# A three-product fp32 split in a transformer trunk: high weights against high and low activations in one product

## The chip, the cores and the metric

One core of one Trainium2 chip. The metric is the device time of one execution in microseconds; the lower the better.

## The reference

A trunk of two layers on one sequence of 256 tokens, width 1024, in float32. Each layer has a mixer with three branches, merged by gates, and then a SwiGLU: dense in layer 0, top 2 of 8 experts in layer 1.

```python
for l in range(DEPTH):
    h = rmsnorm(x, g_mix[l])
    p = h @ w_in[l]
    c_q, c_kv, k_r, z_sg, q_x, gate_logits = jnp.split(p, SPLITS, axis=-1)
    y_a = mla_branch(c_q, c_kv, k_r, ...)          # latent self-attention, 8 heads
    y_b = spatial_gating_branch(z_sg, ...)         # u * (w_s @ rmsnorm(v) + b_s), u, v = split(gelu(z_sg))
    y_c = memory_branch(q_x, mem_n, w_mkv[l])      # 4 heads over 256 memory rows
    yd = jnp.einsum('bsnw,nwd->bsnd', jnp.stack([y_a, y_b, y_c], axis=2), w_br[l])
    gates = jax.nn.sigmoid(gate_logits.reshape(b, s, N_BRANCH, d) + b_gate[l])
    x = x + jnp.sum(gates * yd, axis=2) @ w_out[l]
    h = rmsnorm(x, g_ffn[l])
    x = x + (swiglu(h, ...) if l % 2 == 0 else moe_swiglu(h, ...))
return rmsnorm(x, g_final)
```

## The kernel before, in words

**Precision.** Large weights and their activations are split: the high part is a copy to float32r (ScalarE, L1219), the low part is the value less its high part (VectorE, L1567). A product is the sum of three: high x high, weights high x activations low, weights low x activations high (`acc3`, L594). Activations stand transposed in `hT`, two tiles `hT_hi` and `hT_lo` of 128 x 8 x 256; `mT` and `yT` are alike. In the transposed products (gates, su, qx, dense up) a block of 128 x 128 weights is stationary and 256 tokens move through, three times for each of 8 blocks of rows.

**Weights.** They come in pieces of 1 MB into slots of `raw` (3 slots in the mixer, 7 else), one piece behind the other in the order of `pieces` (L424 on; there `su` is the first half u of the spatial branch's input, `sv` its half v, `qx` the memory branch's query, `gate` and `br` the gates and projections of a branch n, w1, w3, w2 the dense weights). A slot is loaded again when the low part of its old piece is made. `whi` and `wlo` have 3 slots (SPLIT): piece m needs the products of piece m - 3 done. `room(name)` (L534) counts the pieces whose slots come free by marks before the mark of `name`; ScalarE and VectorE call `hi_parts(room(...))` and `lo_parts(room(...))` at fixed places of their in-order programs, and wait there for the release.

**PSUM.** `plan_psum` (L61) hands out the banks at build time: in the mixer six in rotation (0 to 3, 6, 7), in the dense stage four for the up projections. `claim` waits on TensorE until the last group in that bank has been read, `full` waits for a product, `read` for the reader of a bank.

**Order of a layer's mixer on TensorE.** cq, ckv, sv (tokens as rows), then su and qx (`transposed`, L675), spatial matrices, latent transposes, latent products q (L730). Then `mixer_steps` (L156), an order written by hand. Memory attention, i = 0 to 5: scores ms(i), at i = 0 also k and v; transposed probabilities mpT(i - 1), values mo(i - 2), and one unit (1, i). Then transposes qT and kT. Self-attention, i = 0 to 9: scores as(i), apT(i - 1), O(i - 2), and a unit: (1, 6), (1, 7), (2, 0) to (2, 7). Last oT and the units of branch 0, (0, 0) to (0, 7), and the output product.

**A unit** (n, d) (L732) is channel block d of branch n: a gate product of 24 matmuls and a projection of 12, side by side in one bank; gate first, but for d = 3 and 7, where the projection is first. ScalarE takes the tanh of the gate from PSUM (L1326), VectorE merges in the same step: (tanh + 1) x projection (L1733), and for n != 1 adds it to the sum (L1737); for n = 0 it also splits the sum (L1739, L1740). `sig` and the temporary have two buffers. In the memory steps VectorE also makes the row maximum of the scores (L1752), scales the probabilities (L1760), makes the low half of a value (L1771) and rotates the queries and keys (L1716 to L1721).

**Dense stage** (L864): for each b two chunks of 128 hidden channels; a chunk is a w1 and a w3 product in the halves of one bank; silu on ScalarE (L1399), product and split on VectorE (L1842 to L1844); then the down product of block b - 1. Behind it comes the expert stage (L975 to L1007), which takes over half of the time.

## Time and profile before

| what | value |
|---|---|
| median of 3 runs (lowest to highest) | 1710.83 us (1710.59 to 1711.66) |
| profiled execution, own time | 1712.28 us |
| its span, first to last instruction | 1710.5 us |
| mean granted TensorE clock | 0.995 |
| share of the chain that ended last on TensorE | 95% |

The sum of a prediction is made against the profiled execution, 1712.28 us, which is 1.45 us over the median; 1.8 us of it lie around the span. Durations of matmuls in a profile overlap, so the distance between two starts is what one costs in a row.

### The profile page before, as it was taken

What the parts mean: (1) busy time and instruction counts of PE and PEld (TensorE: products, weight loads), DVE (VectorE), ACT (ScalarE), POOL (GpSimd) and SP (SyncE); (2) the same over time, 40 slices, a digit from 0 to 9 for tenths busy, and PEclk for the clock granted to TensorE, in tenths of its full rate; (3) what the DMA queues carried; (4) which work ended last, traced back from release to release, by engine and by line L of the source; (5) the groups of instructions that cost most, each with busy time, mean ns of one, the idle gap of its engine ahead of it and who ended that gap; (6) DMA issues with size and microseconds to landing.
All of it is one profiled execution on the core that took longest, in us unless ns stands there. A gap on an engine that the chain in (4) does not pass through costs nothing.

```text
span 1710.5 us, 24615 instructions
## 1 busy us (share of the span) xinstructions
PE 1668.2 (98%) x9340; PEld 1449.8 (85%) x9340; DVE 1283.9 (75%) x1221; ACT 1051.2 (61%) x965; POOL 18.3 (1%) x44
## 2 busy tenths in 40 slices
PE   7999999999999999999999999999999999999996
PEld 6989998999988999888888888888888888888885
DVE  6655575655565556678888888888888888888996
ACT  5534544433453454457777777777777777777774
POOL 1000000000000000000000000000000000000100
PEclk9999999999999999999999999999999999999998
DMA  8633449885473335769999999999999999999992
GB/s 277 199 123 100 123 148 354 302 262 177 157 219 125 123 115 170 260 244 385 354 388 390 357 387 390 355 397 385 364 393 377 364 392 362 386 391 358 393 394 110
DMA packets 252569, 493.96 MB, mean 289 GB/s; under 512 B 8310, under 2 KB 86720, under 8 KB 252496
## 3 DMA queue, kind: packets, MB, share of 16 engines
q1 hardware_dynamic: 247424, 479.23, 78.3%
q10 hardware_dynamic: 3664, 9.44, 1.4%
q0 software_dynamic: 1408, 4.28, 0.7%
q8 instruction: 50, 0.82, 0.2%
q14 instruction: 23, 0.19, 0.0%
HBM read 473.52 MB, written 19.40 MB: 288 GB/s over the span
## 4 chain that ended last, share of the span: by engine, by line
PE 95%; DVE 2%; issue 1%; ACT 1%; DMA 0%; DVEq 0%; ACTq 0%; SPq 0%
PE bank L601 34%; PE bank L975 24%; PE bank L1007 18%; PE bank L979 12%; PE bank L591 3%; PE bank L992 1%; PE bank L825 1%; PE bank L796 1%; PE bank L639 1%; DVE wlo L1567 0%; PE bank L778 0%; PE bank L1019 0%; PE bank L651 0%; DMA hn<-in_mem 0%; ACT pbuf L1232 0%
## 5 line engine op out<-in xcount | busy, mean ns | idle before, releaser
L1924 DVE TENSOR_TENSOR wlo<-raw,whi 128x2048 fp32r<-128x2048 f32 x328 | 748.1, 2288 | 108.9 <-ACT whi L1432 108.7
L1432 ACT ACTIVATE whi<-raw 128x2048 fp32r<-128x2048 f32 x328 | 627.8, 1919 | 179.5 <-PE bank L979 94.2
L1567 DVE TENSOR_TENSOR wlo<-raw,whi 128x2048 fp32r<-128x2048 f32 (+3 forms) x113 | 249.3, 2210 | 196.7 <-ACT whi L1219 196.5
L975 PE MATMUL bank<-whi,yT_hi 128*128 128x512 f32 x896 | 354.3, 395 | 0.8 <-issue 0.8
L975 PE MATMUL bank<-whi,yT_lo 128*128 128x512 f32 x896 | 349.3, 390 | 0.0
L1219 ACT ACTIVATE whi<-raw 128x2048 fp32r<-128x2048 f32 (+3 forms) x113 | 209.0, 1851 | 131.9 <-PE bank L601 114.1
L601 PE MATMUL bank<-hT_hi,whi 128*128 128x256 f32 x848 | 243.7, 287 | 3.1 <-DVE hT_lo L1589 1.8
L979 PE MATMUL bank<-wlo,yT_hi 128*128 128x512 f32 x896 | 240.0, 390 | 0.0
L601 PE MATMUL bank<-hT_hi,wlo 128*128 128x256 f32 x848 | 239.9, 283 | 0.0
L601 PE MATMUL bank<-hT_lo,whi 128*128 128x256 f32 x848 | 239.8, 283 | 0.0
L979 PEld LDWEIGHTS bank<-wlo,yT_hi 128*128 128x128 f32 x896 | 168.2, 188 | 35.6
L975 PEld LDWEIGHTS bank<-whi,yT_hi 128*128 128x128 f32 x896 | 168.3, 188 | 34.5 <-issue 0.9
L975 PEld LDWEIGHTS bank<-whi,yT_lo 128*128 128x128 f32 x896 | 168.4, 188 | 33.5
L1007 PE MATMUL bank<-whi,yT_hi 128*128 128x512 f32 x448 | 176.4, 394 | 3.4 <-DVE yT_lo L1939 2.4
L1007 PE MATMUL bank<-wlo,yT_hi 128*128 128x512 f32 x448 | 175.2, 391 | 0.0
L1007 PE MATMUL bank<-whi,yT_lo 128*128 128x512 f32 x448 | 175.1, 391 | 0.0
L601 PEld LDWEIGHTS bank<-hT_hi,whi 128*128 128x128 f32 x848 | 162.5, 192 | 4.6 <-issue 2.0
L601 PEld LDWEIGHTS bank<-hT_lo,whi 128*128 128x128 f32 x848 | 162.5, 192 | 1.1 <-issue 0.5
L601 PEld LDWEIGHTS bank<-hT_hi,wlo 128*128 128x128 f32 x848 | 162.4, 192 | 0.0
L1007 PEld LDWEIGHTS bank<-whi,yT_hi 128*128 128x128 f32 x448 | 84.4, 188 | 28.3 <-issue 8.6
L1007 PEld LDWEIGHTS bank<-wlo,yT_hi 128*128 128x128 f32 x448 | 84.5, 189 | 18.0
L1007 PEld LDWEIGHTS bank<-whi,yT_lo 128*128 128x128 f32 x448 | 84.6, 189 | 16.3
(263 smaller groups left out, 1788.7 us busy)
## 6 DMA issues: line engine op xcount, KB each, us to landing
raw<-in_moe_w SPq DMA_DIRECT2D x336, 1024.0 KB, 7.5
raw<-in_w_in SPq DMA_DIRECT2D x36, 1024.0 KB, 5.3
raw<-in_dense_w SPq DMA_DIRECT2D x30, 1024.0 KB, 8.0
raw<-in_w_br SPq DMA_DIRECT2D x12, 1024.0 KB, 5.1
raw<-in_w_mkv SPq DMA_DIRECT2D x8, 1024.0 KB, 6.4
raw<-in_w_out SPq DMA_DIRECT2D x8, 1024.0 KB, 5.0
rows_by_slot<-qxT SPq DMA_DIRECT2D x15, 512.0 KB, 8.8
y_by_slot<-qxT SPq DMA_DIRECT2D x9, 512.0 KB, 8.4
```

The lines of the kernel that those rows point to most:

```text
L591: ins = nc.tensor.matmul(bank, lhs(k), rhs(k), start=(k == 0), stop=(k == n - 1))
L601: ins = nc.tensor.matmul(bank, lhs(a, k), rhs(b, k), start=(start and k == chunks[0] and a + b == 0), stop=(stop and k == chunks[-1] and a ...
L639: nc.tensor.matmul(b[:, 0:P], ident[:, :], ident[:, :], start=True, stop=True)
L796: ins = nc.tensor.transpose(b[:, a:a + P], prob[:, nth % 2, t, tok(kt)], ident[:, :])
L825: ins = nc.tensor.matmul(b[:, t * SEQ:(t + 1) * SEQ], qT[0:QK, h, tok(t)], kT[0:QK, h, :], start=True, stop=True)
L975: nc.tensor.matmul(b[:, :], hselT[a][:, half, tok(k)], w[:, k, :], start=(half + k + a == 0), stop=False)
L979: ins = nc.tensor.matmul(b[:, :], hselT[0][:, half, tok(k)], w[:, k, :], start=False, stop=(half == 1 and k == 3))
L1007: ins = nc.tensor.matmul(banks[4 + n][:, :], gated_m[a][:, tok(2 * half + c)], w[p][:, c, n * HALF:(n + 1) * HALF], start=(b_ + half + c + ...
L1219: nc.scalar.activation(whi[:, m % SPLIT, 0:floats(n)], raw[:, pieces[n][1], 0:floats(n)], ACT.Copy).then_inc(hi_ready, 1)
L1432: nc.scalar.activation(whi[:, (E0 + n) % SPLIT, :], raw[:, n % RAW, :], ACT.Copy).then_inc(hi_ready, 1)
L1567: V.tensor_tensor(wlo[:, m % SPLIT, 0:size], raw[:, pieces[n][1], 0:size], whi[:, m % SPLIT, 0:size].bitcast(F32), ALU.subtract).then_inc( ...
L1924: V.tensor_tensor(wlo[:, s, :], raw[:, n % RAW, :], whi[:, s, :].bitcast(F32), ALU.subtract).then_inc(lo_ready, 1)
```

## The change

The high weights of a block are multiplied with high and low activations at once: the two halves stand side by side in one tile `hT`, and move as 512 columns; the low weights' 256-column product is added to the first half of the bank. A product so fills a whole bank, and VectorE adds the bank's halves into SBUF. This is done for su, qx, the gates and dense w1 and w3. gelu, tanh and silu then read the sum from SBUF. A unit takes two banks, and its merge on VectorE is put behind the work of the next step (`waiting`), in branch 0 behind the next unit's add. `down` waits for the new semaphore `gated_ready`. The views of `hT` for the expert stage are laid out anew. Diff, cut:

```diff
+    def take_unit(l, n, d):
+        for name in ("unit", "gate") if d % 4 == 3 else ("gate", "unit"):
+            take((name, l, n, d))
...
-            for t in range(2):
+            for t in range(4 if name in ("su", "qx") else 2):
                 take((name, l, t))
...
+                take(("up1", l, c), among=(0, 1, 2, 3))
                 take(("up", l, c), among=(0, 1, 2, 3))
...
-        hT = [sb(f"hT_{i}", [P, KD, SEQ], F32R) for i in ("hi", "lo")]
+        hT_both = sb("hT", [P, KD, 2, SEQ], F32R)
+        hT = [hT_both[:, :, i, :] for i in range(2)]
...
+        gate_sum = cT[:, 3:5, :]
...
+            def acc_pair(bank, w, cc, norm=None):
+                for k in range(KD):
+                    if norm is not None and k % 2 == 0:
+                        read(pe, ("nT", norm, k // 2))
+                    nc.tensor.matmul(bank[:, :], w[0][:, k, tok(cc)], hT_both[:, k, :, :].rearrange("p a s -> p (a s)"),
+                                     start=(k == 0), stop=False)
+                    ins = nc.tensor.matmul(bank[:, 0:SEQ], w[1][:, k, tok(cc)], hT[0][:, k, :],
+                                           start=False, stop=(k == KD - 1))
+                return ins
...
-                transposed("su", hT)
-                transposed("qx", hT)
+                for name in ("su", "qx"):
+                    for i in range(4):
+                        if i % 2 == 0:
+                            w = weight((name, l, i // 2), KD)
+                        ins = acc_pair(claim((name, l, i)), w, i % 2)
+                        mark(ins, (name, l, i), *([("piece", name, l, i // 2)] if i % 2 else []))
...
                     def gate():
                         w = weight(("gate", l, n, d // 2), KD)
-                        return acc3(b[:, 0:SEQ], lambda a, k: w[a][:, k, tok(d % 2)], lambda a, k: hT[a][:, k, :],
-                                    range(KD), True, True)
+                        ins = acc_pair(claim(("gate", l, n, d)), w, d % 2)
+                        mark(ins, ("gate", l, n, d), *([("piece", "gate", l, n, d // 2)] if d % 2 else []))
...
@@ ScalarE
-                for n in range(2):
-                    hi_parts(room(("su", l, n)))
-                    b = full(act, ("su", l, n))
...
+                for i in range(4):
+                    hi_parts(room(("su", l, i)))
+                    read(act, ("su", l, i))
+                    nc.scalar.activation(uT[:, i, :], uT[:, i, :], ACT.Gelu_apprx_tanh).then_inc(u_ready, 1)
+                for i in range(4):
+                    hi_parts(room(("qx", l, i)))
...
-                    b = full(act, ("unit", l, n, d))
+                    read(act, ("gate", l, n, d))
...
-                        hi_parts(room(name))
+                        hi_parts(room(("gate",) + name[1:] if kind == "unit" else name))
...
+                        hi_parts(room(("up1", l, c)))
+                        read(act, ("up1", l, c))
+                        nc.scalar.activation(silu_d[:, c % 4, :], silu_d[:, c % 4, :], ACT.Silu).then_inc(silu_ready, 1)
                         hi_parts(room(("up", l, c)))
...
@@ VectorE
+            def add_halves(dst, name):
+                b = full(dve, name)
+                free(V.tensor_reduce(dst, b[:, :].rearrange("p (a s) -> p s a", a=2), AX_X, ALU.add), name)
...
+                for i in range(4):
+                    lo_parts(room(("su", l, i)))
+                    add_halves(uT[:, i, :], ("su", l, i))
+                for i in range(4):
+                    lo_parts(room(("qx", l, i)))
                     if l:
                         dve.wait_ge(zeroed, 16 * N_ZEROED)
-                    free(V.tensor_copy(qxT[:, 2 * n:2 * n + 2, :].rearrange("p h s -> p (h s)"), b[:, :]), ("qx", l, n))
+                    add_halves(qxT[:, i, :], ("qx", l, i))
...
+                def unit_gate(n, d):
+                    lo_parts(room(("gate", l, n, d)))
+                    add_halves(gate_sum[:, (units + len(waiting)) % 2, :], ("gate", l, n, d))
+                    waiting.append((n, d))
+                def merge_waiting():
+                    while waiting:
+                        lo_parts(room(("unit", l) + waiting[0]))
+                        unit_merge(*waiting.pop(0))
...
-                    if kind not in ("O", "ms", "as", "k"):
+                    if kind not in ("O", "ms", "as", "k", "unit"):
                         lo_parts(room(name))
...
-                        unit_merge(*step[1:])
+                        unit_gate(*step[1:])
+                        continue
...
+                    merge_waiting()
+                merge_waiting()
...
                 for d in range(KD):
-                    lo_parts(room(("unit", l, 0, d)))
-                    unit_merge(0, d)
+                    unit_gate(0, d)
+                    if d:
+                        lo_parts(room(("unit", l) + waiting[0]))
+                        unit_merge(*waiting.pop(0))
+                merge_waiting()
...
+                        lo_parts(room(("up1", l, c)))
+                        add_halves(silu_d[:, c % 4, :], ("up1", l, c))
                         lo_parts(room(("up", l, c)))
...
-                        link(V.tensor_tensor(g, silu_d[:, c % 4, :], b[:, SEQ:2 * SEQ], ALU.mult))
+                        add_halves(g, ("up", l, c))
+                        read(dve, ("up", l, c))
+                        dve.wait_ge(silu_ready, c + 1)
+                        link(V.tensor_tensor(g, g, silu_d[:, c % 4, :], ALU.mult))
```

## Rows read from the trace of the kernel before

**Rows 1.** The page, part 1 (busy time) and part 6 (loads, last number us to landing).
```profile
PE 1668.2 (98%) x9340; PEld 1449.8 (85%) x9340; DVE 1283.9 (75%) x1221; ACT 1051.2 (61%) x965; POOL 18.3 (1%) x44
...
raw<-in_w_br SPq DMA_DIRECT2D x12, 1024.0 KB, 5.1
```

**Rows 2.** The chain that ended last, first 760 us (start, length, what; x counts instructions).
```profile
151.68 4.32 PE bank L601 x36
...
156.00 0.87 PE bank L825 x4
...
212.39 56.50 PE bank L601 x384
...
326.25 155.46 PE bank L601 x1068
...
484.82 48.91 PE bank L601 x336
...
537.04 7.84 PE bank L591 x24
```

**Rows 3.** Groups by line and form, the 256-column product of high and high.
```profile
L601 PE MATMUL bank<-hT_hi,whi 128*128 128x256 f32 x848 | 243.7, 287 | 3.1 <-DVE hT_lo L1589 1.8 <-DVE mT_lo L1589 1.3
```

**Rows 4.** TensorE's timeline (start, length, what), 24 products of 512 columns between the two.
```profile
337.84 0.40 PE L601 MATMUL bank<-whi,yT_hi 128*128 128x512 f32 x1
...
343.30 0.28 PE L601 MATMUL bank<-hT_hi,whi 128*128 128x256 f32 x1
```

**Rows 5.** VectorE's timeline, layer 1, around the qx projection.
```profile
519.90 2.28 DVE L1567 TENSOR_TENSOR wlo<-raw,whi 128x2048 fp32r<-128x2048 f32 x1
...
534.64 2.05 DVE L1686 TENSOR_SCALAR cT<-bank,cols 128x256 f32<-128x256 f32 x5 [0.18 <-PE bank L632]
```

**Rows 6.** VectorE's timeline, layer 0, first mixer steps.
```profile
123.98 0.68 DVE L1752 TENSOR_REDUCE rmax<-bank 128x2 f32<-128x512 f32 x1
...
126.79 0.42 DVE L1771 TENSOR_TENSOR yT_lo<-bank,yT_hi 128x256 fp32r<-128x256 f32 x1
...
128.46 0.41 DVE L1733 SCALAR_TENSOR_TENSOR hn<-cT,bank 128x256 f32<-128x256 f32 x1
...
145.18 2.29 DVE L1567 TENSOR_TENSOR wlo<-raw,whi 128x2048 fp32r<-128x2048 f32 x1 [3.78 <-ACT whi L1219]
...
147.39 0.41 DVE L1733 SCALAR_TENSOR_TENSOR hn<-cT,bank 128x256 f32<-128x256 f32 x1
...
147.72 2.47 DVE L1790 COPY raw<-bank 96x512 f32<-96x512 f32 x4
```

**Rows 7.** ScalarE's timeline, the same steps.
```profile
125.82 0.59 ACT L1350 ACTIVATE pbuf<-bank 128x512 f32<-128x512 f32 x1
...
143.24 1.92 ACT L1219 ACTIVATE whi<-raw 128x2048 fp32r<-128x2048 f32 x1 [2.55 <-PE bank L601]
...
145.06 0.46 ACT L1326 ACTIVATE cT<-bank,half_gate 128x256 f32<-128x256 f32 x1
```

**Rows 8.** TensorE's timeline, from the last of these steps to the first attention scores.
```profile
144.42 2.34 PE L815 MATMUL bank<-ident,raw 128*96 128x128 f32 x20
...
147.86 1.84 PE L815 MATMUL bank<-ident,raw 128*96 128x128 f32 x12 [1.10 <-DVE hn L1733]
...
150.58 1.10 PE L825 MATMUL bank<-raw 96*128 96x256 f32 x4 [0.88 <-ACT raw L1363]
```

**Rows 9.** VectorE's timeline, a merge of branch 0 and the operation behind it.
```profile
231.18 0.41 DVE L1733 SCALAR_TENSOR_TENSOR sgv<-cT,bank 128x256 f32<-128x256 f32 x1
...
232.75 2.28 DVE L1567 TENSOR_TENSOR wlo<-raw,whi 128x2048 fp32r<-128x2048 f32 x1
```

**Rows 10.** Waits, first 760 us (us in all, times, longest).
```profile
PE bank L639 <- DVE hT_lo L1589: 3.5, 1, 3.5
```

**Rows 11.** A stretch around 725 us: busy time of PE, PEld, DVE, ACT, POOL, then granted clock.
```profile
720.00:730.00 10.00, 8.78 (x51) 8.59 (x51) 8.99 (x13) 1.54 (x2) 0.00 (x0) 0.68 0.77 283
```

More of the change, by code:

```diff
@@ L95, in plan_psum @@
         for step in mixer_steps(heads, x_heads):
-            if step[0] != "O":
+            if step[0] == "unit":
+                take_unit(l, *step[1:])
+            elif step[0] != "O":
                 take((step[0], l) + step[1:])
@@ L102, in plan_psum @@
         for d in range(8):
-            take(("unit", l, 0, d))
+            take_unit(l, 0, d)
         for n in range(2):
@@ L1299, in _ @@
                 own_squares()
-                for n in range(2):
-                    hi_parts(room(("su", l, n)))
-                    b = full(act, ("su", l, n))
-                    free(nc.scalar.activation(uT[:, 2 * n:2 * n + 2, :].rearrange("p h s -> p (h s)"), b[:, :],
-                                              ACT.Gelu_apprx_tanh), ("su", l, n))
-                for n in range(2):
-                    hi_parts(room(("qx", l, n)))
+                for i in range(4):
[4 more added lines that the diff above has]
+                    hi_parts(room(("qx", l, i)))
                 hi_parts(room(("wsT", l)))
@@ L1371, in _ @@
                 for d in range(KD):
-                    hi_parts(room(("unit", l, 0, d)))
+                    hi_parts(room(("gate", l, 0, d)))
                     unit_tanh(0, d)
@@ L1689, in _ @@
                 dve.wait_ge(row_in, 16 * (l + 1))
-                for n in range(2):
-                    read(dve, ("su", l, n))
+                dve.wait_ge(u_ready, 4 * (l + 1))
                 for t in range(T):
@@ L1727, in unit_merge @@
                     units += 1
+                    b = full(dve, name)
                     dve.wait_ge(tanh_ready, units)
-                    b = banks[groups[name].bank]
                     s_ = sig[:, (units - 1) % 2, :]
@@ L1732, in unit_merge @@
                     dst = mixT[:, d, :] if first else gated_tmp[:, units % 2, :]
-                    free(V.scalar_tensor_tensor(out=dst, in0=s_, scalar=1.0, in1=b[:, SEQ:2 * SEQ], op0=ALU.add,
+                    free(V.scalar_tensor_tensor(out=dst, in0=s_, scalar=1.0, in1=b[:, 0:SEQ], op0=ALU.add,
                                                 op1=ALU.mult), name)
@@ L1836, in _ @@
                             norm_lo(3 * l + 3, mT, c_of["mem"])
+                        lo_parts(room(("up1", l, c)))
+                        add_halves(silu_d[:, c % 4, :], ("up1", l, c))
                         lo_parts(room(("up", l, c)))
-                        dve.wait_ge(silu_ready, c + 1)
-                        b = banks[groups["up", l, c].bank]
                         g = g32_d[:, c % 2, :]
                         part = [v[:, c // BD % 2, c % BD, :] for v in gated_d]
-                        link(V.tensor_tensor(g, silu_d[:, c % 4, :], b[:, SEQ:2 * SEQ], ALU.mult))
+                        add_halves(g, ("up", l, c))
+                        read(dve, ("up", l, c))
+                        dve.wait_ge(silu_ready, c + 1)
+                        link(V.tensor_tensor(g, g, silu_d[:, c % 4, :], ALU.mult))
                         link(V.tensor_copy(part[0], g))
-                        free(V.tensor_tensor(part[1], g, part[0].bitcast(F32), ALU.subtract), ("up", l, c))
+                        V.tensor_tensor(part[1], g, part[0].bitcast(F32), ALU.subtract).then_inc(gated_ready, 1)
             for t in range(T):
```

52 lines of the change are left out of this document (22 added, 30 removed).

## The prediction, made before the changed kernel ran

> **What bounds the kernel.** I read the page first: TensorE has work for 98% of the span, VectorE 75%, ScalarE 61% [rows 1]. So time can be won only on TensorE, or lost where another engine makes it wait. Next the chain that ended last, over the first 760 us, since the expert loop behind them (L975, L1007) is not touched: in the stages that the change edits, the chain is TensorE's own matmuls end to end; the output and branch-0 stage is one piece of 56.50 us, the dense stage one of 155.46 us [rows 2]. The reader should see there that a stage without a wait gives back exactly what its matmuls get shorter by.
>
> Then the price of a matmul. The group row says 287 ns for a 256-column product, x848 [rows 3], but matmuls overlap: the mean is a latency. The price is the distance between starts. 36 products of 256 columns take 4.32 us [rows 2], 0.120 us each; 24 of 512 columns take 343.30 - 337.84 = 5.46 us [rows 4], 0.2275 us each. So 256 more columns cost 0.1075 us, and each product has some 0.0125 us on top.
>
> **TensorE's part.** Each weight block of 128 rows had three 256-column products, 0.360 us. It gets one of 512 and one of 256, 0.3475 us: 0.0125 us less. There are 848 of them [rows 3]: 336 in the dense up projections (42 products of 8 blocks), 384 in the gates (48), 128 in su and qx (16). That is 848 x 0.0125 = **-10.6 us**, 0.10 us a product of 8 blocks. No row shows 512 and 256 columns in turn. Bounds: 0.333 us a pair if one of the two fixed parts goes (-22.9 us), 0.360 if nothing is won (0). I take 0.3475, since both sizes carry the same fixed part when they follow their own kind. The Trainium skill, "TensorE: Matmul & The Clock Gate", section "Back-to-back issue gap", puts an isolated gap at columns/2.4 + 2.5 ns; by it this sum would be 848 x 2.5 ns = 2.1 us, but both measured distances lie over 10 ns above that formula.
>
> **VectorE's part.** Every one of the 106 products gets an add of halves, a reduction over 512 PSUM elements. The nearest row is the maximum of attention scores, same operand size: 0.68 us long [rows 6], and four copies of this length come every 0.62 us [rows 6]. I take 0.62. Bounds: 0.33, the distance behind a 256-element operation (147.39 to 147.72) [rows 6], and twice 0.68 if the strided read of pairs is slow. qx loses two copies of 0.62 a layer. What counts is where the add stands: ScalarE's tanh, gelu and silu now wait for it, and behind them in ScalarE's queue stand high parts of weights (1.9 us [rows 7]), then in VectorE's queue their low parts (2.2 us from start to start [rows 6]), for which TensorE waits. No DMA is added or moved by itself, but a load waits for the low part of the piece in its slot.
>
> *Dense up projections.* A block of two chunks is 4 x 2.78 + 5.46 = 16.6 us on TensorE. VectorE has 3 x 2.2 low parts, 4 adds, two chains of 1.1: 11.3 us. The first weights' next piece is freed at 8.3 us; add, silu, high and low part end at 13.7, before it is wanted at 16.6. The second pair's is ready 1.7 us early. Four banks hold two chunks. Added work is hidden; cover left is those 1.7 us. Full gain, -4.2 us.
>
> *su and qx.* VectorE is held by the normalisation of v until 519.90 [rows 5]; su's first two products are long done, so adds run at 519.9 to 521.2, gelu to 521.6, and only then ScalarE makes qx's second high part (to 523.5), VectorE its low part (to 525.7). TensorE wants it at 527.3: no wait. But su's other adds and gelus end at 527.4, the first gate piece's high part at 529.3, low part at 531.5, qx's first two adds at 532.7. The first projection piece loads into the slot whose low part ended at 525.7, so 5.1 us later [rows 1]: high part 531 to 533, low part to 535.2, two adds to 536.5. The five latent copies, 2.05 us [rows 5], end at 538.6, and the latent products, which read them and started at 537.04 [rows 2], start at 538.8: **1.8 us later**, the 0.8 us gained included, so 2.6 us of stall.
>
> *First mixer steps, with memory scores.* Two banks a unit instead of one, of six in rotation, and the merge is put behind the next step's scores. Let 0 be the start of the third scores (ms2). TensorE: scores 0.87 [rows 2], transposes, values, gate to 5.0, projection to 6.4; then ms3 wants the bank of unit (1,1). VectorE: maximum to scaled probabilities is 126.79 - 123.98 = 2.8 us [rows 6]; ScalarE is free 1.84 after the maximum started [rows 7], makes the high part freed by gate (1,1) until 4.6, VectorE the low part until 6.9, the merge until 7.3: **0.9 us wait**. Then VectorE runs solid: yT and rotation 1.67 [rows 6], add, ms3's 2.8, merge, yT and rotation, low part to 16.5, add (1,3) to 17.2, tanh 0.46, high part to 19.5, low part to 21.8, merge (1,3) to 22.2. TensorE is at the last values (mo3) at 19.25 and wants just that bank: **3.0 us wait**. Last, gate (1,5) ends at 25.9; VectorE reaches its add at 27.0; tanh, high part, low part, a copy and the merge end at 32.7. TensorE finished five groups of transposes in 2.34 us [rows 8] at 29.65: a wait of 3.05 where 1.10 stood [rows 8]; the scores then follow 0.5 us sooner after it, since copies overlap (before, 150.58 - 147.86 [rows 8]). Stall added: 0.9 + 3.0 + 1.95 - 0.5 = **5.3 us**.
>
> *Self-attention steps.* A step is 6.4 us on TensorE and about 4.3 on VectorE. The same chain makes VectorE at most 2.5 us late, and every bank comes free before its next claim. Nothing added.
>
> *Branch 0.* A unit is 4.2 us on TensorE; on VectorE the merge is 232.75 - 231.18 = 1.57 us [rows 9], add 0.62, three quarters of a low part 1.65: 3.85 us. Played through, it begins with 0.65 us for oT's low half, which now stands behind add and tanh, and ends with the last merge 0.6 us after TensorE wants it: **1.25 us**.
>
> **Sum.** Stalls 2 x (2.6 + 5.3 + 1.25) = 18.3 us, less 10.6: +7.7 us. The profiled execution took 1712.28 us (span 1710.5), so 1720.0; the median of the runs, 1710.83, gives **1718.5 us**. If adds cost 0.33, some six in su and qx, four in the steps and one in branch 0 leave the path, 11 x 0.29 x 2 = 6.4 us: +1.3. If they cost 1.36, +16 more.
>
> **Rivals.** *A: the stalls don't come* because my order of queues is too strict or adds are short. For it: in the dense stage cover is there; against: VectorE already has no gap from 126.79 to 128.46 and behind. Then 1710.83 - 10.6 = 1700.2 us; with half the stalls 1709. Faster by over 0.2% (3.4 us, what a measurement can tell from no change): 0.20, within it 0.13. *B: the clock falls.* The 3.5 us wait [rows 10] was followed by 10 us at a mean granted clock of 0.68, so 6.4 us of them at 1.2 GHz instead of 2.4 [rows 11]; mo3's wait and kT's, four of some 3 us in all, come near it. At 1.2 GHz 256 columns take twice their 0.107, 0.213 us, so such a fall costs 6.4 x (1 - 0.120/0.213) = 2.8 us; after two of the four: 1718.5 + 5.6 = 1724.1. Chance 0.15. *C: no product saving*, the fixed part following columns when sizes alternate: 1718.5 + 10.6 = 1729.1, chance 0.05. The skill's formula above would give 1718.5 + 8.5 = 1727; it is worth 0.02 more, as the rows contradict it.
>
> **Numbers.** My forecast has 0.45 (its own range 1714.3 to 1723), B, C and the formula 0.22, A's faster side 0.20, no change 0.13: slower 0.67. The range, 1702 to 1726, reaches into A up to nearly all its gain and takes in B; outside it stay C and a full A.
>
> **What would show it.** Right: in su, gates and up the two products start 0.347 us apart in pairs; the dense stage is 4.2 us shorter; TensorE waits for merge L1733 or its successor at ms3, mo3 and kT; the latent products start late behind qx's adds. Wrong: adds of under 0.4 or over 1 us, pairs of other length, dense stage with waits, or no wait of TensorE between 92 and 151 us.

## The result, and the profile after

The changed kernel takes 1733.04 us, the median of 4 runs (1732.85 to 1734.85), beside 1710.71 for the kernel before (1709.48 to 1711.66): ratio 1.0132, 95% interval 1.012 to 1.0145, **22.3 us slower**. The sign was forecast; 1718.5 us and the range up to 1726 were too low. The profiled executions differ alike: a span of 1731.3 us beside 1710.5. Of the version best_fill below, one of eleven executions took 3529.7 us; its median, 1708.35, counts it (1707.8 without), its ratio doesn't.

The page of the kernel after: busy time of each engine, with its share of the span.

```profile
PE 1666.3 (96%) x8492; PEld 1404.7 (81%) x8492; DVE 1347.0 (78%) x1323; ACT 1052.9 (61%) x969; POOL 18.1 (1%) x44
...
PE 87%; DVE 7%; ACT 3%; issue 3%; DMA 0%; DVEq 0%; ACTq 0%; SPq 0%
...
L622 PE MATMUL bank<-hT,whi 128*128 128x512 f32 x848 | 308.2, 405 | 3.2 <-DVE hT L1617 1.8
...
L624 PE MATMUL bank<-hT,wlo 128*128 128x256 f32 x848 | 239.1, 282 | 0.0
...
L1348 ACT ACTIVATE cT<-cT,half_gate 128x256 f32<-128x256 f32 x48 | 24.5, 510 | 131.2 <-DVE cT L1597 131.2
```

TensorE, which had work for 98% of the span [rows 1], now has it for 96%. L622 is the wide product, L624 the narrow one, L1597 the add of halves. VectorE and ScalarE together hold a tenth of the chain that ended last, the chain of work in which each piece released the next. ScalarE's tanh stands idle 131 us for the adds; that costs nothing by itself, but weights' high parts are queued behind it.

TensorE's waits of the kernel after, us in total, times and longest:

```profile
PE bank L938 <- DVE qxT L1907: 6.2, 1, 6.2
PE bank L840 <- DVE hn L1774: 5.7, 2, 2.8
PE bank L603 <- DVE hn L1774: 5.5, 2, 2.7
...
PE bank L613 <- DVE yT_lo L1852: 3.1, 2, 1.5
...
PE bank L803 <- DVE hn L1774: 2.0, 2, 1.0
```

Once a layer, TensorE waits for a merge (L1774) at kT (L840, where 1.1 us stood before [rows 8]), at the last value product mo3 (L603), and at the fourth memory scores (L803): the three places forecast. L613 is branch 0's first projection; L938, at the router, comes up in the section on the router.

Where the time went, from the start of the first product of each stage in both traces (`cq` is the first product of a layer's mixer, q the latent products). Both layers are summed; a forecast is stalls less saved product time:

| stage | change, us | forecast |
|---|---|---|
| up to cq of layer 0 | -1.6 | 0 |
| cq to the start of q, with su and qx | +3.0 | +3.6 |
| memory steps, qT and kT, to the first scores | +14.8 | +9.4 |
| self-attention steps | -0.6 | -2.0 |
| branch 0 and output | +4.8 | +0.9 |
| dense stage | -1.9 | -4.2 |
| end of layer 1's output to the first expert | +1.2 | 0 |
| experts | +1.2 | 0 |
| sum | +20.8 | +7.7 |

The experts stage, which no version touches, took between 956.4 and 959.5 us in the traces of this study; differences of its size are no effect. The same holds for the stretch from the first product with weights (15.1 us) to cq of layer 0, which took 26.4 to 28.2 us in this study: in the kernel before TensorE starts 15 products between 14 and 18 us, in the one after 25, at a granted clock of 1.00 in both. Why isn't settled.

### The profile page after: what moved, and what is told of

The parts are those of the page before. It is cut to its first block, busy times and chain, and to the rows that moved or that the text cites. A ratio compares the mean times of both kernels' runs of the same rounds, so it can differ in the third digit from the quotient of the medians.

```text
span 1731.3 us, 23163 instructions
## 1 busy us (share of the span) xinstructions
PE 1666.3 (96%) x8492; PEld 1404.7 (81%) x8492; DVE 1347.0 (78%) x1323; ACT 1052.9 (61%) x969; POOL 18.1 (1%) x44
## 4 chain that ended last, share of the span: by engine, by line
PE 87%; DVE 7%; ACT 3%; issue 3%; DMA 0%; DVEq 0%; ACTq 0%; SPq 0%
PE bank L998 23%; PE bank L1030 18%; PE bank L613 14%; PE bank L1002 12%; PE bank L622 9%; PE bank L624 4%; PE bank L603 3%; ACT whi L1242 2%; DVE wlo L1590 2%; PE bank L1015 1%; PE bank L850 1%; PE bank L821 1%; DVE cT L1597 0%; PE bank L662 0%; DVE pbuf L1597 0%
## 5 line engine op out<-in xcount | busy, mean ns | idle before, releaser
L622 PE MATMUL bank<-hT,whi 128*128 128x512 f32 x848 | 308.2, 405 | 3.2 <-DVE hT L1617 1.8
L624 PE MATMUL bank<-hT,wlo 128*128 128x256 f32 x848 | 239.1, 282 | 0.0
L622 PEld LDWEIGHTS bank<-hT,whi 128*128 128x128 f32 x848 | 160.8, 190 | 41.9 <-DVE wlo L1590 2.3
L624 PEld LDWEIGHTS bank<-hT,wlo 128*128 128x128 f32 x848 | 161.7, 191 | 1.1 <-issue 0.5
L1348 ACT ACTIVATE cT<-cT,half_gate 128x256 f32<-128x256 f32 x48 | 24.5, 510 | 131.2 <-DVE cT L1597 131.2
L1463 ACT ACTIVATE sgv<-bank 128x512 f32<-128x512 f32 x56 | 33.6, 599 | 44.8 <-PE bank L1002 44.7
```

Of the source, the lines that this page charges most:

```text
L622: nc.tensor.matmul(bank[:, :], w[0][:, k, tok(cc)], hT_both[:, k, :, :].rearrange("p a s -> p (a s)"), start=(k == 0), stop=False)
L624: ins = nc.tensor.matmul(bank[:, 0:SEQ], w[1][:, k, tok(cc)], hT[0][:, k, :], start=False, stop=(k == KD - 1))
L1463: free(nc.scalar.activation(silu_m, b[:, :], ACT.Silu), (phase, "e1", b_))
```

## One part at a time: dense, gates, su and qx

The theory going in: TensorE bounds, the stalls come from VectorE's adds and their place in the queues, and the three parts add up. Its rivals: the saving per pair is off, the clock falls cost what is missing, or the parts disturb one another.

```diff
 # dense_only: only these stay as in the change
+    ins = acc_pair(b, w1, cc, ...)
+    ins = acc_pair(b, w3, cc)
 # dense_grouped: besides, in acc_pair
     for k in range(KD):
         nc.tensor.matmul(bank[:, :], w[0][:, k, tok(cc)], hT_both[:, k, :, :]..., start=(k == 0), stop=False)
+    for k in range(KD):
         ins = nc.tensor.matmul(bank[:, 0:SEQ], w[1][:, k, tok(cc)], hT[0][:, k, :], ...)
```

> The 512 + 256 pair and the add of halves in the dense up projections alone; su, qx and gates as before. Theory 1 (the loss sits in the mixer, where adds, high parts and merges stand in line; a pair is 0.353 us and not 0.3475): the dense stage is 336 x 0.007 = 2.3 us shorter, TensorE waits nowhere new, total -1.9 to -2.4 us, ratio 0.9987. Theory 2 (the adds also cost in the dense stage, and the mixer is only part of the loss): 0 to +5 us. Theory 3 (pairs at 0.3475): -4.2 us, ratio 0.9975.

1707.75 us, ratio 0.9984 (0.9975 to 0.9993): faster by 2.9 us. The interval reaches from 1.2 to 4.3 us, so the total can't tell theory 1 from theory 3; the distances in the trace do. Only the dense stage moved. Its part behind the sixth chunk, 240 pairs, became 1.65 us shorter, 0.0069 us a pair, which is theory 1's price. TensorE's rows of one gate in the kernel after show it, here its last four pairs, in order of time:

```profile
209.78 0.40 PE L622 MATMUL bank<-hT,whi 128*128 128x512 f32 x1
210.01 0.28 PE L624 MATMUL bank<-hT,wlo 128*128 128x256 f32 x1
210.12 0.40 PE L622 MATMUL bank<-hT,whi 128*128 128x512 f32 x1
...
210.84 0.40 PE L622 MATMUL bank<-hT,whi 128*128 128x512 f32 x1
211.07 0.28 PE L624 MATMUL bank<-hT,wlo 128*128 128x256 f32 x1
211.19 0.28 PE L613 MATMUL bank<-yT_hi,whi 128*128 128x256 f32 x1
```

Four pairs take 211.19 - 209.78 = 1.41 us, 0.353 each, where 0.3475 was forecast. Over the whole trace the median distance from a wide product's start to the narrow one's is 236 ns, from narrow to the next wide 117.

> As dense_only, but each product runs its eight 512-column matmuls first and then its eight 256-column ones. If the excess of a pair over 0.3475 us comes from alternating sizes (236 + 117 ns where uniform rows show 227 and 120), distances go back to 227 and 120 inside each run of eight and 336 x 0.0055 = 1.8 us more are won than in dense_only: about -4 us. If the excess belongs to the 512-column matmul on the joined tile itself, distances stay at 236 and 117 and the time is that of dense_only.

1707.23 us, ratio 0.9982 (0.9973 to 0.9991). Two groups of eight in this kernel:

```profile
347.03 2.00 PE L621 MATMUL bank<-hT,whi 128*128 128x512 f32 x8
348.87 1.11 PE L624 MATMUL bank<-hT,wlo 128*128 128x256 f32 x8
349.82 2.00 PE L621 MATMUL bank<-hT,whi 128*128 128x512 f32 x8
```

(349.82 - 347.03) / 8 = 0.349 us a pair; eight wide ones alone 1.84 / 8 = 0.230. The same part of the stage is 2.74 us shorter, 0.0114 a pair. So equal widths in a row keep nearly the price of uniform rows, and the change of width within the pair cost the difference. The two totals can't be told apart; the stage shows it. Both kernels lose 0.8 and 1.5 us in the first six chunks, where the granted clock fell for 3.4 us at 278 us behind the norm's wait, and did not in the kernel before. So the traced executions show less of the gain than the medians; that of dense_only was the longest of eleven, 1710.66 us.

```diff
 # gates_only: the change's gates and their merge order; dense, su, qx as before
+    ins = acc_pair(claim(("gate", l, n, d)), w, d % 2)
```

> Pair, add, two banks a unit and late merge for the gates alone; su, qx and dense as before. Theory 1: the waits at ms3, mo3 and kT, those around branch 0 and the clock falls behind them are all here: 2 x (1.1 + 2.9 + 1.7) + 2 x 2.6 in waits, 3 clock falls of 1.5, less 384 x 0.007 = 2.7: +18 to +20 us of the +22, ratio 1.011. Theory 2: well under half of it, below +11.

1729.92 us, ratio 1.0114 (1.0099 to 1.013), 19.3 us slower than before. Per layer: memory steps +5.4, transposes +1.5, self-attention -0.3, branch 0 +1.2, its last units and the output +1.3. **The gates are nearly the whole loss**, and their waits are those of the full change:

```profile
PE bank L834 <- DVE hn L1771: 5.7, 2, 2.8
PE bank L602 <- DVE hn L1771: 5.6, 2, 2.9
...
PE bank L612 <- DVE yT_lo L1849: 3.1, 2, 1.5
```

```diff
 # suqx_only: the change's su and qx stage; gates and dense as before
+                for name in ("su", "qx"):
+                    for i in range(4):
+                        ins = acc_pair(claim((name, l, i)), w, i % 2)
```

> Pair and add for su and qx alone. Theory 1: latent products start 1.5 us later in each layer, nothing else moves: +3.0 us, ratio 1.0018. Theory 2 (part of a loss spread over all): +7 or more. If the late VectorE there was harmless: -0.9 us.

1715.32 us, ratio 1.0027 (1.0018 to 1.0036). Per layer the products give back 0.4 us, and q starts 1.9 us later after them. The router's stretch costs another 1.6, taken up below. The three parts alone differ from the kernel before by -2.9, +19.3 and +4.7: 21.1, and together +22.3. Within the intervals they add up.

```diff
 # suqx_early: ScalarE, su and qx
                 for i in range(4):
                     hi_parts(room(("su", l, i)))
-                    read(act, ("su", l, i)); gelu(uT[:, i, :])
                 for i in range(4):
                     hi_parts(room(("qx", l, i)))
+                for i in range(4):
+                    read(act, ("su", l, i)); gelu(uT[:, i, :])
```

> The su and qx pairs alone, with ScalarE's high parts ahead of the gelus. In the run without that order the stretch from the spatial transposes to q took 5.3 us a layer where the kernel before takes 3.3. Theory 1 (VectorE waited for high parts behind the gelus): the stretch is back at 3.4 or shorter, the total about 1711.4. Theory 2 (VectorE's own work sets it): the stretch stays at 5.3, the total 1715.3 as before.

1712.41 us, ratio 1.0007 (0.9998 to 1.0017). The stretch from the spatial transposes to q is back at 3.34 us in both layers, where it was 5.3. So the gelus, each behind an add, had held back high parts, these the low parts, and those the adds of qx. The edit needs no engine to be faster. The forecast's stall is undone by order alone.

## The gates: order, banks, the length of the add

```diff
 # now_late: the merge in its own step; the units' low parts stay behind it
-                        lo_parts(room(("unit", l) + waiting[0]))    # now_late alone
 # now_early: the unit's low parts ahead of the merge, its high parts ahead of the gate's
+                        if kind == "unit": hi_parts(room(name))
                     elif kind == "unit":
                         unit_gate(*step[1:])
-                        continue
 # banks8: all groups of the memory steps, qT and kT take turns over eight banks
+        how = {"among": (0, 1, 2, 3, 6, 7, 4, 5)}
 # short_add: the add is a copy of the bank's first half
-  V.tensor_reduce(dst, b[:, :].rearrange("p (a s) -> p s a", a=2), AX_X, ALU.add)
+  V.tensor_copy(dst, b[:, 0:SEQ])
```

> The changed kernel with one part undone: in the memory and self-attention steps a unit is merged in its own step again, right behind its add (pieces' high and low parts stay where they are; branch 0 as changed). Theory 1a (TensorE waits for banks that a late merge frees): the waits at ms3 (1.1 us a layer) and kT's bank go, mo3's falls from 2.9 to about 1.7 us, where it then waits for the copy of mpT3 behind a high part: 2.3 us a layer, and the clock falls behind mo3 with it: -5 to -9 us against the changed kernel. Theory 1b (the late merge protects the score chain; the loss is VectorE's and ScalarE's queue alone): no gain, or up to +3 us.

1746.38 us, ratio 1.021 (1.0181 to 1.024), 13 us **slower** than the change. The memory steps gained 3.1 us a layer, the self-attention steps lost 8.8. Of these 2.5 are in the first step, where the granted clock is 0.50 for 10.2 us in layer 0 and 6.8 in layer 1, behind kT's wait of 3.6 us; 6.2 are in the last three, with another fall of 6.8 us. There the merge waits on VectorE for its own tanh, and the row maximum of the next scores stands behind it. The trace of this kernel around one step:

```profile
203.15 0.42 DVE L1773 SCALAR_TENSOR_TENSOR sgv<-cT,bank 128x256 f32<-128x256 f32 x1 [0.71 <-ACT cT L1348]
...
203.60 0.42 DVE L1777 TENSOR_TENSOR hn<-hn,sgv 128x256 f32<-128x256 f32 x1
...
204.06 0.69 DVE L1792 TENSOR_REDUCE rmax<-bank 128x2 f32<-128x512 f32 x1
...
206.07 0.66 PE L821 MATMUL bank<-ident,pbuf 128*128 128x128 f32 x4 [1.30 <-ACT pbuf L1364]
```

Merge, its sum, maximum, exponentials, and TensorE waits 1.30 us to transpose them. The change's late merge is right there, as now_early shows without a fall; how much of the 6.2 us here is the fall isn't shown.

> As now_late, and ScalarE makes the high part that a gate frees before it waits for that gate's add, VectorE the low part before the merge, as it was before the change. Theory 1a and the order of queues together: ms3 0, mo3 1.7, kT back to 1.3 us of wait: 4 us a layer and two or three clock falls of 1.5 us: -8 to -12 us against the changed kernel. If the order of high parts doesn't matter: the time of now_late.

1732.15 us, ratio 1.0127 (1.0098 to 1.0157): 4.1 us a layer gained in the memory steps, 3.5 us lost in self-attention in layer 1, without any fall of the clock, and 5.1 in layer 0, of which 1.7 are in the first step, in a fall that starts at 150.5 us. So order alone costs some 3.5 us a layer there. Same total, other places.

> The changed kernel with eight banks in rotation instead of six in the memory steps, nothing else. Theory 1a: the bank waits go exactly as with now_late (ms3 0, mo3 1.7 us behind mpT3's copy), although VectorE's order is untouched: -5 to -9 us against the changed kernel. Theory 1b: the banks are not the matter, waits only change their name: within 1 us.

1733.5 us, ratio 1.0135 (1.0106 to 1.0164). The wait at the fourth scores is gone and the memory steps are 3.8 us a layer shorter, but the one at kT is 4.6 us instead of 2.8 (9.3 us in the two layers), and the self-attention steps take 2.0 more, all of it in the first: 7.25 us instead of 5.20. A fall of the granted clock covers it (stretch, length, busy time of the engines, then the PE clock, 0.50):

```profile
153.40:160.20 6.80, 5.48 (x16) 4.32 (x17) 2.91 (x6) 1.61 (x5) 0.00 (x0) 0.50 0.52 154
```

Two more banks move a wait, and VectorE's work stays; what the longer wait adds behind it is the clock.

> The changed kernel with the add of halves replaced by a copy of the first half (the products' high x low part is left out of the output): the same places and waits, a shorter VectorE operation, about 0.33 instead of 0.62 us. Theory 1 by my sum: 11 adds a layer stand on the path, 11 x 0.29 x 2 = -6.4 us, more if clock falls go. If place and not length matters: -2 us or less.

1724.82 us, ratio 1.0084 (1.0055 to 1.0114); it leaves out the product of high weights and low activations. Its copy took 0.42 us, the real add 0.68:

```profile
L1597 DVE COPY cT<-bank x48: 416/418/425, 114.3 to 701.9; 128x256 f32<-128x256 f32 x48
```

0.26 us less for each of 106 adds gives 8.2 us of the median, so the length of the add matters too: 1.0 a layer in su and qx, 2.1 in the memory steps, 1.5 in branch 0. Most of the loss stays with an add of half the bank.

```diff
 # mem_now: own-step merges and early high parts in the six memory steps alone
+                        if kind == "unit" and step[1] == 1 and step[2] < 6:
+                            hi_parts(room(name))
...
                         unit_gate(*step[1:])
-                        continue
+                        if step[1] > 1 or step[2] > 5:
+                            continue
```

> The changed kernel, with the merge in the unit's own step and the branch weights' high parts ahead of the gate's in the six memory steps alone; the self-attention steps keep the late merge. Theory 1 (the waits of 2.7 to 3.1 us at the last mo and at kT are for banks whose merge stands behind a 2.3 us low part, which is late behind tanh and the high part; with both earlier they go, and the 4 to 9 us that the runs with this order everywhere lost came from the self-attention steps alone): from the first unit to the qT steps 4.1 us less a layer, nothing lost behind them: 1725. Theory 2 (VectorE is the bound there and the wait moves on to kT or the first scores): 4.1 us less and 2 to 4 more behind, 1729 to 1733.

1725.29 us, ratio 1.0091 (1.0076 to 1.0106), 7.8 less than the change: theory 1's number. Memory steps -4.2 and -4.0 us; the self-attention steps are unchanged in layer 1, and 1.7 us longer in layer 0, where the clock falls for 6.8 us from 150.7. What held TensorE at mo3 in the change is seen on VectorE and ScalarE there:

```profile
137.00 0.68 DVE L1597 TENSOR_REDUCE cT<-bank 128x256 f32<-128x512 f32 x1
...
140.13 2.29 DVE L1590 TENSOR_TENSOR wlo<-raw,whi 128x2048 fp32r<-128x2048 f32 x1 [2.44 <-ACT whi L1242]
142.34 0.42 DVE L1774 SCALAR_TENSOR_TENSOR hn<-cT,bank 128x256 f32<-128x256 f32 x1
```

```profile
137.78 0.51 ACT L1348 ACTIVATE cT<-cT,half_gate 128x256 f32<-128x256 f32 x1 [3.18 <-DVE cT L1597]
138.19 1.90 ACT L1242 ACTIVATE whi<-raw 128x2048 fp32r<-128x2048 f32 x1
```

Add, tanh, high part, low part, and only then the merge that frees the bank: 142.34 - 137.00 = 5.3 us from the add to the merge, of which VectorE idles 2.44. The tanh was ready at 138.3; the merge could have been made before the low part. With the order changed, mo3's wait falls to 1.4 us, and it is then ScalarE's:

```profile
PE bank L840 <- DVE hn L1776: 5.0, 2, 2.5
...
PE bank L603 <- ACT pbuf L1374: 2.8, 2, 1.4
```

kT's stays near 2.5, so theory 2 is right about that one wait.

```diff
 # oT_first: the merge that is left after the last step goes behind oT's low parts
-                merge_waiting()
                 for n in range(2):
                     b = full(dve, ("oT", l, n))
...
+                merge_waiting()
```

> The changed kernel with the merge that is still waiting after the last self-attention step put behind the low parts of oT on VectorE. Theory 1 (that merge and the low parts of weights ahead of it are what holds branch 0's first product back): the 1.1 us a layer between oT and out go, 1731. Theory 2 (the wait is ScalarE's, whose high parts of oT come late): nothing, 1733.

1732.75 us, ratio 1.0127 (1.0112 to 1.0142). The stretch from oT to out became 0.42 us a layer shorter, not 1.1, and the total can't be told from the change's. The wait of branch 0's first projection for oT's low part is still 1.28 us where it had been 1.70. What is left stands on VectorE and ScalarE in this kernel:

```profile
217.56 1.92 ACT L1242 ACTIVATE whi<-raw 128x2048 fp32r<-128x2048 f32 x1 [1.79 <-PE bank L613]
219.58 2.29 DVE L1590 TENSOR_TENSOR wlo<-raw,whi 128x2048 fp32r<-128x2048 f32 x1 [1.88 <-ACT whi L1242]
221.79 0.68 DVE L1597 TENSOR_REDUCE cT<-bank 128x256 f32<-128x512 f32 x1
222.57 0.51 ACT L1348 ACTIVATE cT<-cT,half_gate 128x256 f32<-128x256 f32 x1 [3.09 <-DVE cT L1597]
222.99 1.07 ACT L1391 ACTIVATE yT_hi<-bank 128x512 fp32r<-128x512 f32 x2
223.67 1.29 DVE L1851 TENSOR_TENSOR yT_lo<-bank,yT_hi 128x512 fp32r<-128x512 f32 x2 [1.19 <-ACT yT_hi L1391]
```

High part, low part, the last unit's add, its tanh, and only then ScalarE's copy of oT, for which VectorE idles 1.19 us. So theory 2 holds for the larger part: it is ScalarE's, which is held by tanh, and tanh by the add. The merge was worth 0.4 us.

```diff
 # pairs_grouped: the full change with dense_grouped's order in acc_pair, for all 106 products
```

> The changed kernel with all 106 groups of eight pairs issued as eight wide products and then eight narrow ones. Theory 1 (the change of width within a pair costs TensorE 0.0045 us, as the dense stage showed, and TensorE is the bound everywhere but at its waits): -3.7 us, about 1729.3. Theory 2 (in the memory steps and at branch 0 VectorE is what TensorE waits for, so those 256 pairs give nothing): -2.7 us, about 1730.4. Theory 3 (the dense stage's gain has another cause than the alternation): 1733, no difference, and the distances stay at 236 and 117 ns in the gates.

1731.33 us, ratio 1.0123 (1.0107 to 1.0138): 1.7 us less, less than either theory gave. The dense stage behind its sixth chunk gains 1.33 us; su and qx gain 0.26 a layer and q starts 0.25 to 0.41 later after them; in the memory steps and the transposes of layer 0 nothing changes. Where VectorE's adds decide, shorter products give nothing. The traces differ in two falls of the clock as well: this one has one at 286.7 us, which costs the first six chunks 1.6 us, and lacks the one at 604.3.

## The clock

In the change the granted clock behind mo3's wait is half, shown by windows of this stretch (columns: stretch, length, busy time of PE, PEld, DVE, ACT and POOL, PE clock, DMA share, GB/s):

```profile
135.00:140.00 5.00, 5.00 (x33) 4.50 (x32) 2.68 (x2) 2.22 (x2) 0.00 (x0) 1.00 0.33 97
140.00:143.50 3.50, 0.76 (x5) 0.58 (x4) 3.34 (x8) 0.84 (x3) 0.00 (x0) 1.00 0.44 163
143.50:147.00 3.50, 3.50 (x12) 2.93 (x11) 2.42 (x13) 0.78 (x2) 0.00 (x0) 0.51 0.97 290
```

TensorE had 0.76 us of work in 3.5 us, and in the next 3.5 the clock was 0.51, 1.2 GHz instead of 2.4, while the next gate ran. Rival B had named this place, with a fall twice as long.

```diff
 # filled: in the bank of the product itself, ahead of the wait for its input
+    b = claim(name)
+    for _ in range(20): nc.tensor.matmul(b[:, 0:P], ident, ident, start=True, stop=True)
     read(pe, ("mpT", l, h))      # and alike before kT
 # filled4: in bank 4, ahead of the claim
+    keep_clock(("o", l, 0), 11)
```

> The changed kernel with 20 products of the identity with itself (109 ns each) ahead of TensorE's two 2.9 us waits in each layer (the last mo and the first kT); their banks are claimed first and overwritten. Theory 1 (rival B of the prediction: the granted clock falls behind these idle stretches and the 3.4 us at the lower level cost 1.0 to 1.5 us each): no fall near 143.5, 594.1 and 604.3 us, the gate behind mo in its usual time, the total 3 to 4 us lower, about 1729.5. Theory 2 (the falls have another cause, or cost nothing as TensorE would wait anyway): the total stays at 1733 within 0.7 us.

1742.96 us, ratio 1.0192 (1.0176 to 1.0207): 10 us slower. The wait at mo3 moved to the identity products, with 2.6 us each time:

```profile
PE bank L826 <- DVE hn L1778: 5.3, 2, 2.6
```

So mo3's wait is for the **bank**, not for the input, and the products came behind it: 20 of them are 40 passes of 0.109 to 0.115 us, 4.6 us each time, added to the path. Before kT they ran without a wait, since TensorE was that much later, so for kT this run doesn't tell bank from input. A miss as a test of the clock, but it settled what mo3 waits for.

> The changed kernel with 11 products of the identity (two passes of 109 ns each, 2.4 us in all) ahead of TensorE's waits at the last mo and at the first kT of each layer, in bank 4, which no memory step uses, so that they run during the wait for the bank and not behind it (the last such run claimed the bank first, had 20 products there, and they came behind the wait). Theory 1 (the granted clock falls behind these idle stretches, and that costs 1.0 to 1.5 us each time): no fall near 143.5, 594.1 and 604.3 us, the total about 3 us lower, 1730. Theory 2 (the falls come anyway, or cost nothing since VectorE is what TensorE waits for): the total within 0.7 us of 1733.

1732.45 us, ratio 1.0123 (1.0108 to 1.0138): by the median only 0.6 us less. The trace says more. The same stretch, with TensorE kept busy:

```profile
140.00:143.50 3.50, 3.50 (x32) 3.46 (x31) 1.63 (x1) 2.59 (x4) 0.00 (x0) 1.00 0.87 301
143.50:147.00 3.50, 3.23 (x21) 2.79 (x20) 3.36 (x18) 0.00 (x0) 0.00 (x0) 1.00 0.47 121
...
545.00:550.00 5.00, 4.96 (x19) 3.47 (x19) 4.96 (x15) 0.00 (x0) 0.00 (x0) 0.66 0.00 0
```

No fall behind mo3 in either layer. (The traces of now_late, now_early, banks8, mem_now and short_add have none there either, so some 1.1 us a layer of what these gain in the memory steps is the clock.) From the first unit to the first scores it took 1.14 us less in layer 0 and 2.24 in layer 1, 3.4 in all for the three falls that the change's trace has there (143.5, 594.1 and 604.3 us): 1.1 us a fall. But another came at 545.7 us, behind a wait of 2.2 us before q, and from cq to the first unit layer 1 took 2.4 us more. Only 1.0 of them lie behind the start of q, in the fall; 1.4 lie ahead of it, where a high part on ScalarE waited 2.85 us for the load of a branch weight, instead of 1.51:

```profile
539.43 1.92 ACT L1244 ACTIVATE whi<-raw 128x2048 fp32r<-128x2048 f32 x1 [2.85 <-DMA raw<-in_w_br]
```

The first stretch of the profiled execution, where executions differ anyway, was 1.7 us longer. So theory 1 holds for a single fall, and the total doesn't show it. Which wait is followed by a fall differs between executions: oT_first is the same program as the change up to oT, and its falls start at 145.2, 155.4 and 595.7 us, those of the change at 143.5, 594.1 and 604.3. From qT to the first scores it took 8.86 us in layer 0 and 7.66 in layer 1, the change 7.67 and 8.84.

## The router, and the version that beats both

```diff
 # best: dense_grouped and suqx_early together; gates as before
 # best_fill: besides, on TensorE ahead of the router's wait
             b = claim(("logits", l))
+            keep_clock(("logits", l), 24)
             read(pe, ("logT", l))
```

> The grouped dense stage (eight wide products, then eight narrow ones) together with the su and qx pairs, ScalarE making all of their high parts ahead of the four gelus; the gates as in the kernel before. Theory 1 (the stages add up, and the later start of q in the run with su and qx alone comes from VectorE waiting for high parts behind the gelus): dense -3.4 us as measured, su and qx -0.4 us a layer with q's delay gone, the router stage +1.6 as measured: about 1708, ratio 0.9985. Theory 2 (VectorE's own low parts and adds delay q, whatever ScalarE's order): q 1.9 us late a layer again, 1712, ratio 1.0006.

1709.15 us, ratio 0.9992 (0.9983 to 1.0001). The interval takes in 1, so it isn't shown to be faster than the kernel before. At the router's sums it was 5.0 us ahead of the kernel before, at the first expert 2.75. Its TensorE rows there, and the mask on VectorE:

```profile
724.27 0.38 PE L941 MATMUL bank<-ident,qxT 8*128 8x8 f32 x2 [6.22 <-DVE qxT L1891]
724.58 5.07 PE L662 MATMUL bank<-ident 128*128 128x128 f32 x24
...
726.79 0.17 DVE L1905 TENSOR_TENSOR mask<-hot 128x16 f32<-128x16 f32 x1
...
729.49 0.29 PE L947 MATMUL bank<-mask,lower 128*128 128x8 f32 x2
```

The mask was ready at 727.0. TensorE was still in its 12 clock-keeping products (24 passes), which took 5.07 us after the 6.2 us of idling; in the kernel before, whose 3.5 us wait [rows 10] stood earlier, before the router's products, they took 2.9:

```profile
720.71 4.61 PE L639 MATMUL bank<-ident 128*128 128x128 f32 x20 [3.48 <-DVE hT_lo L1589]
...
729.45 2.94 PE L639 MATMUL bank<-ident 128*128 128x128 f32 x24
```

The wait moved: before, the clock-keeping products ahead of the router's waited for the norm's hT_lo, and the router's products came late; now they start at 712.8 without a wait, and TensorE is through early. The plan hands banks out in turn, and su and qx take four more groups a layer, so the norm's third group no longer lies in bank 6, the router's. No run tried this by itself, but the traces sort by it: with the third group in bank 6 (before, dense_only, dense_grouped, gates_only) these products start 10.3 us after those of the norm, in the fifteen others 6.7 to 6.9. The bank isn't the only cause of slow products ahead of the mask's: in gates_only the wait stands where it did, a fall starts at 747.3 us, and they take 4.6 us.

> The grouped dense stage and the su and qx pairs as in the last best run, with 24 products of the identity (5.2 us) ahead of TensorE's 6.2 us wait for the copy of the router's sums. In that run TensorE came out of this wait at the lower clock, and its 12 clock-keeping products ahead of the mask's took 5.07 us where they take 2.94 in the kernel before, so that the mask's products, whose input was ready at 727.0, started at 729.4. Theory 1: they start at 727.1, the total 2.3 us lower, about 1706.8, ratio 0.9977. Theory 2 (the clock is low there whatever TensorE does): 1709.1.

1708.35 us, ratio 0.9983 (0.9973 to 0.9992), **faster than both kernels**:

```profile
716.90 5.52 PE L662 MATMUL bank<-ident 128*128 128x128 f32 x48
723.27 0.28 PE L942 MATMUL bank<-ident,qxT 8*128 8x8 f32 x2 [0.84 <-DVE qxT L1892]
723.49 2.94 PE L662 MATMUL bank<-ident 128*128 128x128 f32 x24
...
725.70 0.18 DVE L1906 TENSOR_TENSOR mask<-hot 128x16 f32<-128x16 f32 x1
726.27 0.29 PE L948 MATMUL bank<-mask,lower 128*128 128x8 f32 x2
```

The stretch from the router's sums to the first expert is 2.23 us shorter than in best, as forecast. The intervals of best and best_fill overlap, so the totals don't show the difference; the stretch does. dense_grouped alone stands at 1707.23; the two can't be told apart.

```diff
 # repaired: the whole change with grouped pairs, suqx_early, mem_now, oT_first and the router's products
```

> The whole change with everything that the runs so far found to give time back: wide products grouped, all high parts of the su and qx stage ahead of the gelus, own-step merges in the memory steps, oT's low part ahead of the last merge, 24 products of the identity in the router's wait. Summed from the runs that had one of them each (1733.0; grouped -1.7, su and qx -3.8, memory steps -7.1 to -8.8, oT -0.8, router -2.2): 1716 to 1717.5, ratio 1.0035, still behind the kernel before by what VectorE's adds cost at kT, in the self-attention steps and at branch 0. If the gates' pairs were worth having once their order is right, it would come below 1708.4, the time without them.

1717.02 us, ratio 1.0035 (1.0022 to 1.0049), the sum of the single runs. Against best_fill, the same kernel without the gates' pairs and with their old order, it loses 1.2 us a layer in the memory steps, 2.3 and 1.5 in the two layers at kT, 1.9 a layer in branch 0 and the output product, and wins back 0.4 a layer in self-attention. Of the change's 22.3 us 16 are gone: some 14 by the order of work, 2.2 by the products added in the router's wait. The gates' pairs still lose in the best order found.

## Why the prediction was right in sign and wrong in size

Three steps failed: the price of a pair (0.3475 us, measured 0.353), the clock left out of the forecast behind TensorE's waits (three falls, 3.4 us), and the two waits of branch 0 (1.25 us a layer, measured 2.86). The queues and the places of the waits were right.

- **The pair's price** was mis-sized: "0.3475, since both sizes carry the same fixed part when they follow their own kind". They don't follow their own kind here. 0.353 us measured, and 0.349 where they do. That is midway to rival C's 0.360. 848 x 0.0055 = 4.7 us, as an upper bound for what it cost, since grouping, which wins back most of it a pair, gave only 1.7 us of the total. In the dense stage it is 1.8 us of the 2.3 between -1.9 and -4.2; the trace of the change has no fall of the clock there, and 0.5 us stay open. The bound of 0.333 us for a lost fixed part was a slip in the sum: 0.3475 - 0.0125 is 0.335.
- **The add of halves**: right, 0.68 us long, like the contiguous reduction it was read from, so reading strided pairs from PSUM cost nothing extra. Two in a row start 0.60 us apart. The 0.62 was 2.47 us of four copies divided by four, which counts the end of the last one.
- **su and qx**: q 1.8 us later a layer was forecast, 1.5 came, as 1.9 of stall for 2.6 and 0.4 of gain for 0.8; and by the queue order named, as suqx_early shows.
- **Memory steps**: waits of 0.9, 3.0 and 3.05 us were forecast at the fourth scores, mo3 and kT; 1.16, 2.90 and 2.99 came (in layer 0, distance between starts beyond a product's own). kT's is 1.73 more than before, where 1.95 were forecast. The row of the table came out 5.4 us over the forecast all the same, and the step that failed is that the clock stays up behind these waits, which was left to **rival B**: its mechanism came, with three falls of 1.1 us where the rival had two of 2.8. That is 3.4 us; the pair's price is 96 x 0.0055 = 0.5. The scores were to follow 0.5 us sooner behind kT's wait and came 0.22 sooner (157.30 - 154.80 for 150.58 - 147.86), 0.6 in two layers; 1.0 us of the row stays open.
- **Self-attention**: right but for one delay of 0.4 us a layer, ahead of the transposes at 188.5 us in layer 0; the rest is the smaller saving.
- **Branch 0**: "0.65 us for oT's low half, which now stands behind add and tanh" was 1.70, and the last merge's 0.6 was 1.16. The place and the mechanism were right, the size was not: the late weight's low part ahead of the add makes the add itself late. With the narrower saving this is 3.9 us of the 13 missed in the traces.
- **Outside the edited stages** nothing was forecast; the bank rotation moved the router's wait, and the stretch to the first expert took 1.2 us more in the trace of the change, 1.6 in that of best. This was missed: a part that the diff does not touch is still touched by the turn of the banks.

## What to carry to other kernels

On an engine with an in-order queue, an added operation costs what stands behind it, and not its length alone: 0.68 us adds held up 1.9 us high parts, 2.3 us low parts and then bank releases. Order gave back some 14 of 22 us, adds shorter by 0.26 us gave 8. A saving on the bounding engine counts only where no one else delivers its inputs or banks just in time; here that was the dense stage, and there the change pays. Price a product in the sequence that it will have: a 512 and a 256 in turn cost 0.353 us, not the 0.3475 of two uniform rows. And look at the granted clock behind every new wait before a loss is put down to the queue.

## What was not expected of the hardware

Alternating widths: 236 ns for the 512-column product when a 256-column one follows, 227 to 230 when its own kind does, while 256 columns stay at 117 to 120. Clock-keeping products right behind an idle stretch (6.2 us) ran at the lower level themselves here, 5.07 us for 2.94, and held up the work that they should speed up; put into the idle stretch they didn't. And the clock's falls of the trace come behind different waits of 2 to 3 us in different executions, and a fall taken away at one place came back at another. Behind the 4.6 us waits of banks8 a fall lasted 6.8 us and cost 2.0 in the next step; those behind the 3 us waits of the change lasted 3.4 us and cost 1.1.
